# Query, key and state space input projections in upper and lower parts ahead of the state space, and two value tiles ahead of its output

## The reference

```
z = x @ w_in[i]
u_pool, q, k, v, u_ssm = jnp.split(z, splits, axis=-1)        # 256, 384, 384, 384, 384 columns
y_pool = pool_mixer(u_pool, w_pool[i], pool_scale[i])
y_attn = chunk_attention(q, k, v, rel_bias[i])                 # 6 heads of 64
y_ssm = s5_mixer(u_ssm, ...)                                   # complex-diagonal state space, GELU, gate
heads = concat(rms_norm(y_pool), rms_norm(y_attn), rms_norm(y_ssm))
h = layer_norm(DN_ALPHA * x + heads @ w_out[i])
ffn = moe(h, route(h, w_router, router_bias), ...)             # top 2 of 16 experts
ple = sigmoid(h @ w_ple_gate[i]) * (p[i] @ w_ple_proj[i])
x = layer_norm(DN_ALPHA * h + ffn + ple)
```

## Time and profile before

| | us |
|---|---|
| median of three runs | 456.39 |
| lowest and highest | 455.49, 456.59 |
| the profiled execution, device time | 456.71 |
| its span in the trace | 454.9 |
| PE busy in it | 439.2 (97%) |
| DVE, ACT, POOL busy | 335.7, 223.5, 116.2 |
| mean granted clock of PE | 0.993 |

### The profile page before, as it was taken

How to read it: one execution, slowest core, us unless ns; L and a number is a source line. 1 busy time by engine, 2 the same in 40 slices (tenths; PEclk the granted TensorE clock), 3 DMA queues, 4 the chain that set the end, 5 groups by cost and what they waited for, 6 DMA issues and landing times.

```text
span 454.9 us, 5417 instructions
## 1 busy us (share of the span) xinstructions
PE 439.2 (97%) x1933; PEld 297.3 (65%) x1933; DVE 335.7 (74%) x515; ACT 223.5 (49%) x367; POOL 116.2 (26%) x146
## 2 busy tenths in 40 slices
PE   8999999999999999999999999999999999999992
PEld 4444664487676556677687767777777777777651
DVE  3699969885536989998484165778878776789677
ACT  3110461051987850215101155788887777789522
POOL 7880042470056500000007410122212222111200
PEclk9999999999999999999999999999999999999997
DMA  8995023235992981111930239999999999840583
GB/s 273 382 377 161 0 41 87 46 99 152 409 385 72 316 305 46 48 46 55 398 149 2 34 108 424 406 423 418 415 394 369 365 368 371 328 204 20 210 224 139
DMA packets 37049, 103.15 MB, mean 227 GB/s; under 512 B 16028, under 2 KB 22092, under 8 KB 30240
## 3 DMA queue, kind: packets, MB, share of 16 engines
q1 hardware_dynamic: 27728, 91.68, 53.2%
q0 software_dynamic: 5600, 9.44, 6.6%
q10 hardware_dynamic: 3696, 1.71, 1.4%
HBM read 95.39 MB, written 17.86 MB: 249 GB/s over the span
## 4 chain that ended last, share of the span: by engine, by line
PE 70%; DVE 12%; DMA 11%; ACT 4%; issue 1%; SPq 1%; DVEq 0%
PE bank L1298 8%; PE bank L1114 6%; PE bank L946 6%; PE bank L1125 5%; PE bank L1270 5%; DMA region_b<-in_w_exp_down 4%; PE bank L1275 4%; PE bank L1279 4%; PE bank L1283 4%; PE bank L1197 3%; PE bank L1199 3%; PE bank L1198 3%; PE bank L1211 3%; DMA region_b<-in_ssm_par 3%; PE bank L1254 2%; DMA region_b<-expert_scratch 2%
## 5 line engine op out<-in xcount | busy, mean ns | idle before, releaser
L946 PE MATMUL bank<-region_e,region_a 128*128 128x512 f32 x128 | 56.0, 596 | 0.0
L946 PEld LDWEIGHTS bank<-region_e,region_a 128*128 128x128 f32 x128 | 24.0, 190 | 29.7 <-issue 28.7
L1275 PE MATMUL bank<-gate_up_upper,tokens_upper 128*128 128x512 f32 x96 | 36.3, 459 | 0.0
L1114 PE MATMUL bank<-region_b,region_e 128*128 128x512 f32 x68 | 32.9, 607 | 0.0
L568 POOL DMA_INDIRECT slot_scratch<-region_h,slot_i x8 | 8.4, 1054 | 87.2 <-issue 87.2
L581 POOL DMA_INDIRECT expert_scratch<-region_g,region_h x8 | 10.0, 1256 | 80.0 <-ACT region_g L892 80.0
L1823 DVE TENSOR_TENSOR gate_up_lower<-region_a,gate_up_upper 128x1024 fp32r<-128x1024 f32 x24 | 28.0, 1221 | 3.3 <-ACT gate_up_upper L865 3.3
L1279 PE MATMUL bank<-gate_up_upper,tokens_lower 128*128 128x512 f32 x96 | 29.8, 392 | 0.0
L1197 PE MATMUL bank<-ple_gate_upper,hidden_upper 128*128 128x512 f32 x64 | 26.6, 415 | 0.0
L865 ACT ACTIVATE gate_up_upper<-region_a 128x1024 fp32r<-128x1024 f32 x24 | 23.7, 1056 | 3.2 <-DMA region_a<-in_w_exp_down 3.2
L1199 PE MATMUL bank<-ple_gate_upper,hidden_lower 128*128 128x512 f32 x64 | 25.0, 391 | 0.0
(11 more groups left out here) (346 smaller groups left out, 1073.1 us busy)
## 6 DMA issues: line engine op xcount, KB each, us to landing
region_a<-in_w_exp_gate SPq DMA_DIRECT2D x8, 1024.0 KB, 8.1
region_a<-in_w_exp_up SPq DMA_DIRECT2D x8, 1024.0 KB, 17.9
region_a<-in_w_exp_down SPq DMA_DIRECT2D x8, 1024.0 KB, 17.7
region_a<-in_w_in SPq DMA_DIRECT2D x3, 1536.0 KB, 16.6
region_b<-in_w_out SPq DMA_DIRECT2D x1, 4096.0 KB, 14.6
expert_scratch<-zero_scratch SPq DMA_DIRECT2D x8, 512.0 KB, 10.1
region_b<-in_w_exp_gate SPq DMA_DIRECT2D x4, 1024.0 KB, 10.1
region_b<-in_w_exp_up SPq DMA_DIRECT2D x4, 1024.0 KB, 17.6
```

The lines of the kernel that those rows point to most:

```text
L946: last = mm(bank[bank_i][:], w[:, k, m * P:(m + 1) * P], xT[:, k, :], start=(k == 0), stop=(k == KD - 1))
L1114: last = mm(bank[WO_AT[half][group]][:], hdT[:, k, t * P:(t + 1) * P], w_o[:, k, half * 512:half * 512 + 512], start=(i == 0), stop=(i == ...
L1275: mm(out_, x_hi[r][:, k * P:(k + 1) * P], w_hi[:, k], start=False, stop=False)
```

## The change

It has five parts.

1. The projection of `u` and the six query and key tiles keep their first two k-steps in f32 and do the other six in three split matmuls each (`u_term`, `qk_split`). ACT writes the upper parts of x (three pieces of 128x1024), of the weights of `u` (three of 128x768), of the query weights (one of 128x2304) and of the key weights (three of 128x768). DVE writes the lower parts in the same sizes, some in place of the f32 weights.
2. FIRST_K has one piece more (`x_in4`); the query weights have a semaphore of their own and are loaded ahead of the state space's parameters `par`.
3. All six query and key tiles stand ahead of the first scores. The pool tiles take the places of tile q1 and of tile q2, and two value tiles stand where tile k2 stood, ahead of `y`. Banks are dealt out anew.
4. The clearing of `m0` on POOL and the last three doublings of the rotation table stand behind the last key tile and the kernel inputs (`kern_in`); `rot_ready` counts to three.
5. On DVE the normalising of heads 0 and 1 stands behind the scan and no longer ahead of the rotation, and that of head 4 behind the GELU's input. On ACT the copies of value tiles, `y`, probabilities, the exponentials and GELU stand in another order.

The diff, cut to its core:

```diff
-FIRST_K = (0, 1, 2, 4, KD)
-QK_ORDER = (("q", 0), ("k", 0), ("q", 1), ("q", 2), ("k", 1), ("k", 2))
+FIRST_K = (0, 1, 2, 4, 6, KD)
+QK_ORDER = (("q", 0), ("q", 1), ("q", 2), ("k", 0), ("k", 1), ("k", 2))
...
+            load(w_q, w_in_v[:, :, POOL_W:POOL_W + ATT_W], "wq_in")
             load(par[:, C_BRE:SSM_COLS], io["ssm_par"][:, C_BRE:SSM_COLS], "par_in")
-            load(w_q, w_in_v[:, :, POOL_W:POOL_W + ATT_W], "wqk_in")
...
-            link(g.memset(m0, 0.0))
...
             while m < NC:
+                if m == 8:
+                    gp.wait_ge(S["rb_in"], 16)
+                    g.memset(rbias[0:64, :, 192:256], NEG).then_inc(S["rot_ready"], 1)
+                    gp.wait_ge(S["pe_qk"], 6)
+                    g.memset(m0, 0.0).then_inc(S["rot_ready"], 1)
+                    gp.wait_ge(S["kern_in"], 4)
...
+            for i in range(3):
+                ac.wait_ge(S[f"x_in{2 + i}"], 32)
...
+                a.activation(ux_hi[...], xT[:, k, :], ACT.Copy).then_inc(S["xw_hi_set"], 1)
+                a.activation(uw_hi[...], w_ssm[:, k, :], ACT.Copy).then_inc(S["xw_hi_set"], 1)
+            ac.wait_ge(S["wq_in"], 16)
+            a.activation(qw_hi[:], w_q[:, 2:KD, :], ACT.Copy).then_inc(S["xw_hi_set"], 1)
...
+            v_copy(0)
+            v_copy(1)
+            ac.wait_ge(S["s_moved"], 64)
+            y_copy(0)
             exps(2)
+            y_copy(1)
             exps(3)
...
+            y_copy(2)
+            v_copy(2)
             pt_copy(0)
             pt_copy(1)
+            exps(4)
+            exps(5)
+            v_copy(3)
+            pt_copy(2)
             for m in range(3):
                 ac.wait_ge(S["yin_ready"], m + 1)
...
-            v_copy(2)
-            pt_copy(2)
             pt_copy(3)
...
+            def u_term(i, w, x, stop=False):
+                for m in range(3):
+                    for k in (2 * i, 2 * i + 1):
+                        last = mm(bank[m][:], w[...], x[...], start=False, stop=(stop and k == 5))
...
+            def qk_split(n, w, w_hi, w_lo, width, parts):
+                for k in range(2):
+                    mm(dst, w[:, k, m * P:(m + 1) * P], xT[:, k, :], start=(k == 0), stop=False)
+                pe.wait_ge(S["xw_hi_set"], parts)
+                for x in (ux_hi, ux_lo):
+                    for k in range(6):
+                        mm(dst, w_hi[m][...], x[:, k * T:(k + 1) * T], start=False, stop=False)
+                pe.wait_ge(S["xw_lo_set"], parts)
+                for k in range(6):
+                    last = mm(dst, w_lo[...], ux_hi[:, k * T:(k + 1) * T], start=False, stop=(k == 5))
...
-            normalise(0)
-            normalise(1)
-
             dv.wait_ge(S["pe_x"], 1)
-            dv.wait_ge(S["rot_ready"], 1)
+            dv.wait_ge(S["rot_ready"], 3)
...
+            normalise(0)
+            normalise(1)
             add_bias(2)
             add_bias(3)
```

More of the change, by code:

```diff
@@ L77 @@
 X_BANKS = ((3, 7), (0, 6))
-V_BANKS = (7, 1, 2, 5)
+V_BANKS = (7, 0, 7, 5)
 PM_BANKS = (7, 0)
@@ L320, in _ @@
             xv = io["xT"].rearrange("(p k) t -> p k t", k=KD)
-            for i in range(4):
+            for i in range(5):
                 ks = slice(FIRST_K[i], FIRST_K[i + 1])
@@ L951, in _ @@
                 mm(bank[7][:, 0:P], ones[:], ones[:], start=True, stop=True)
[L953 to L955 removed]
+            for k in range(2):
+                pe.wait_ge(S[f"x_in{k}"], 32)
                 for m in range(3):
[L957 to L959 removed]
+                    mm(bank[m][:], w_ssm[:, k, m * P:(m + 1) * P], xT[:, k, :], start=(k == 0), stop=False)
+            def u_term(i, w, x, stop=False):
+                for m in range(3):
+                    for k in (2 * i, 2 * i + 1):
+                        last = mm(bank[m][:], w[:, k * SSM_W + m * P:k * SSM_W + (m + 1) * P], x[:, k * T:(k + 1) * T],
+                                  start=False, stop=(stop and k == 5))
+                    if stop:
+                        last.then_inc(S["pe_u"], 1)
+            for i in range(3):
+                pe.wait_ge(S["xw_hi_set"], 2 * i + 2)
+                u_term(i, uw_hi, ux_hi)
+                pe.wait_ge(S["xw_lo_set"], 2 * i + 1)
+                u_term(i, uw_hi, ux_lo)
+                pe.wait_ge(S["xw_lo_set"], 2 * i + 2)
+                u_term(i, uw_lo, ux_hi, i == 2)
             def qk(n):
@@ L1031, in weigh_values @@
                 last.then_inc(S["pe_pv"], 1)
-            pe.wait_ge(S["wqk_in"], 32)
-            qk(0)
-            qk(1)
-            pe.wait_ge(S["wup_in"], 16)
-            project(POOL_BANKS[0], w_up, 0, "pe_pool")
+            pe.wait_ge(S["wq_in"], 16)
+            for n in range(3):
+                qk_split(n, w_q, [qw_hi[:, m * P:] for m in range(3)], qw_lo, ATT_W, 7)
+            pe.wait_ge(S["wqk_in"], 16)
             pe.wait_ge(S["uT_done"], 3)
-            pe.wait_ge(S["qk_done"], 2)
+            for n in range(3, 6):
+                qk_split(n, w_k, kw_hi, kw_lo, P, n + 5)
+            pe.wait_ge(S["qk_done"], 4)
             scores(0)
@@ L1076, in _ @@
             pe.wait_ge(S["gp_in"], 16 * (4 + CH * 2))
-            for m, (signal, count) in enumerate([("xrot_done", 1), ("pool_in_done", 2), ("qk_done", 6)]):
+            for m, (signal, count) in enumerate([("v_done", 1), ("v_done", 2), ("xrot_done", 1)]):
                 pe.wait_ge(S[signal], count)
```

108 lines of the change are left out of this document (65 added, 43 removed).

## The result

| | before | after |
|---|---|---|
| median, us | 456.31 (5 runs) | 475.70 (5 runs) |
| lowest and highest | 455.35, 456.59 | 475.52, 476.39 |
| span of the profiled execution | 454.9 | 473.7 |
| mean granted clock of PE | 0.993 | 0.958 |

The ratio is 1.0437, with a 95% interval of 1.0422 to 1.0451: 19.4 us slower. The forecast was 461.4, slower by 5.0, in a range up to 464.4. The sign held and the size did not.

The account below looks back on a forecast made before the run. PE was taken as the bound, with nearly full ACT deciding the stage's end. Median 456.39 plus 3.2 us of later gate plus 1.8 us for one clock fall gave 461.4 us, range 454.8 to 464.4.

Parts of the forecast that it names:

- The split: In u and six tiles on PE, three split matmuls take 0.696 us against 0.870 per k-step: 9.4 us less.
- The lower parts: DVE's lower parts, covered by PE's upper-by-upper matmuls, cost nothing; without that cover, up to 1 us each piece.
- POOL's table: Rotation table ready at 74.8 to 76.4, before products end at 77.7; if disturbed, rotation starts 1.2 us later.
- The state chain: Rotation, scan and states' move ahead of y: 23.2 us against 20.5 of PE filler, so PE idles 2.7 us.
- The clock: Idle pieces of 4.4 and 2.9 us ahead of the gate lower PE's clock once, costing 1.8 us; chance 0.43.
- the wait of 2.9 us ahead of the gate: PE's transposes of head 5 wait some 2.9 us for ACT's copies of head 4.
- ACT's list in the tail: Behind y, ACT's work from 119.6 to 140.4 sets the gate's start at 139.4, 3.2 us later than 136.2.
- more than one fall, 463.2: Rival: idle at the opening or ahead of y costs another 1.8 us; chance 0.10, shared with a late table.
- That PE and not ACT sets the gate: Rival: ACT's list 7 us shorter, gate at 132.7, total 452.8; faster by over 0.3% had chance 0.14.

Follow-up runs that it names:

- the run in f32: The changed kernel's order, banks, loads and waits, but the state space projection and six query and key tiles wholly in f32: 483.18 us.
- the late pool tile in the old order: Pool tile in the kernel before with two extra DVE multiplications ahead of the rotation and four dummy matmuls ahead of y: 465.57 us.
- the kernel before with late states: The kernel before with two extra 128x3072 multiplications on DVE ahead of the rotation, so that the states come later: 475.58 us.

## Why the prediction was wrong

- **The split** held: 0.870 against 0.232 x 3 a k-step, u at 25.0, products ending at 77.8, and the run in f32 measured 7.5 us for a sum of 7.1. The lower parts, put at nothing, cost one wait of 0.63 us.
- **POOL's table** held: ready at 76.96 before the products ended at 77.8, nearly at the undisturbed rate.
- **The state chain** was right as the bound in the middle, and mis-sized by 2.9 us: the prediction took rotation and scan at the 16.4 us of the earlier trace rows, and looked for POOL's contention only in the table. It did not ask what POOL does next, beside the last six steps. They run 2.9 us longer.
- **The clock** is the step that failed. The prediction named an idle stretch of 2.7 us ahead of y and put its fall among the rivals, at 1.8 us. That price came from the opening, 3.4 us of 128-column matmuls, behind which the first matmuls of u run at full pace. The profile's clock prints 1.00 over that stretch too, so its low level rests on the pace alone. The price is right for a fall ahead of wide matmuls: 1.7 us ahead of the late pool tile in the old order. The prediction took it for whatever stands behind the wait. y is 20.7 us of 64-column matmuls, busy throughout, and the clock did not come back in it: 9.9 us, and 1.2 in the scores behind it. The sum also left the fall ahead of y out without a reason: for the wait of 2.9 us ahead of the gate it took the 2.1 us at full clock of the earlier trace rows as exceeded, for 2.7 us ahead of y it did not, and behind 2.75 us y ran at 0.50.
- **ACT's list in the tail** held in kind and size: 21.0 us from the transposes of head 0 to the gate, against 20.0, with waits of 4.2 and 1.5 us. Its clock fall was real, 1.6 us of it in the gate, but taking it out gave 0.2 us and not 1.8, since POOL's squares were nearly as late.
- **The rivals**: more than one fall, 463.2, was the nearest. That PE and not ACT sets the gate fell. What none of them had was a fall that lasts for a whole stage, and so the range ended 11 us too low.

## What to carry to other kernels

Before a change that opens a wait, look at what stands behind the wait on PE: a fall of the clock doubles the time of whatever follows until the clock comes back. Here that was 1.7 us ahead of a tile of 512-column matmuls and 9.9 us ahead of y, in which the clock never came back. Take the price from rows of the same kind of matmul as stands behind the wait. Two edits that are sound by themselves, faster tiles and a changed order, can between them uncover a chain that the slow tiles had covered; count the cover in microseconds after the change and not before it. And where an engine's queue is pushed to another time, ask of every later piece in it what it will now run beside.

## What the runs showed of the hardware

- 96 records of f32 matmuls with 64 moving columns, PE busy 20.65 of 20.65 us, ran at a granted clock of 0.50 from the first to the last, in the changed kernel and in the kernel before with late states (20.59 of 20.60 us). Entered at full clock they ran at 1.00 to the end, in 10.8 us, in all traces but one, where the clock fell 2.3 us into them, behind 0.84 us of idle.
- Idle stretches of 2.75, 3.5 and 5.2 us ahead of them ended at the low level. In traces with 1.0 us of wait, and with none, y ran at full clock.
- Behind a wait of 3.2 us ahead of an f32 tile of 512 moving columns the clock stayed at 1.00 in one trace and fell in another, where it was back within 5 us; the tile took 8.83 and not 7.13 us.
- Adding 4.35 us of unused matmuls in the stretch ahead of y took 11.9 us off the kernel.
- Six equal DVE steps with two SBUF operands took 8.6 us beside POOL's additions and 5.7 without; POOL's addition over 128x1022 elements took 3.41 us there.
